# A hybrid decoder step on Trainium2: the opening rearranged, and the dt chain moved between the first blocks of group 0

## The reference

```python
xn = rms_norm(x, norm_mix_w)
u = xn @ w_in                       # 1024 x 10272
glu_v, glu_g, z, xbc, dt_raw, gate_logit = split(u)
a = glu_v * sigmoid(glu_g); a = conv31(a); ...            # convolution branch
xbc = silu(conv4(xbc))                                    # x, B, C of the SSD mixer
dt = softplus(dt_raw + dt_bias)     # 32 heads
A = -exp(a_log)
y, h = ssd(x, dt, A, B, C, h0)      # cumulative sums of dt*A, chunk by chunk (128 tokens)
...
out = (gate0 * y_a + gate1 * y_b) @ w_o
x = x + out; x = x + hier_moe(rms_norm(x))                # 32 experts, top 2
```

## Time and profile before

| | |
|---|---|
| median of 3 runs | 1772.03 us (1767.18 to 1772.23) |
| span of the profiled execution | 1770.0 us |
| TensorE (PE) busy | 1465.9 us, 83% |
| VectorE (DVE) busy | 1348.9 us, 76% |
| ScalarE (ACT) busy | 727.2 us, 41% |
| GpSimd (POOL) busy | 395.0 us, 22% |
| mean granted TensorE clock | 0.903 |

### The profile page before, as it was taken

How to read it: one execution, slowest core, us unless ns; L and a number is a source line. 1 busy time by engine, 2 the same in 40 slices (tenths; PEclk the granted TensorE clock), 3 DMA queues, 4 the chain that set the end, 5 groups by cost and what they waited for, 6 DMA issues and landing times. The chain is left out here.

```text
span 1770.0 us, 27567 instructions
## 1 busy us (share of the span) xinstructions
PE 1465.9 (83%) x8979; PEld 1283.1 (72%) x8979; DVE 1348.9 (76%) x2060; ACT 727.2 (41%) x1012; POOL 395.0 (22%) x467
## 2 busy tenths in 40 slices
PE   3898988989889899898998499998338888888880
PEld 2896887968879688796887389986336777676760
DVE  4169888888888888888888636442738999999984
ACT  3132232322323223232232322332028888888871
POOL 1035243352433424334252000000130000000002
PEclk9599897998989989899799699999669999999995
DMA  4031241411414115141160644320359999999966
GB/s 135 24 96 32 79 107 49 130 44 50 135 47 121 54 45 140 40 128 54 42 179 13 202 143 151 120 78 12 105 210 370 369 372 370 370 371 373 369 241 226
DMA packets 187558, 274.00 MB, mean 155 GB/s; under 512 B 11196, under 2 KB 149670, under 8 KB 172118
## 3 DMA queue, kind: packets, MB, share of 16 engines
q1 hardware_dynamic: 174638, 231.85, 40.0%
q10 hardware_dynamic: 8672, 27.86, 4.0%
q0 software_dynamic: 4208, 13.78, 2.2%
HBM read 224.19 MB, written 50.12 MB: 155 GB/s over the span
## 5 line engine op out<-in xcount | busy, mean ns | idle before, releaser
L731 PE MATMUL pu<-xh,wh 128*128 128x304 f32 (+1 forms) x1280 | 289.2, 309 | 5.8 <-ACT zc L651 4.6
L731 PE MATMUL pu<-xl,wh 128*128 128x304 f32 (+1 forms) x1280 | 279.8, 301 | 0.0
L731 PE MATMUL pu<-xh,wl 128*128 128x304 f32 (+1 forms) x1280 | 278.1, 300 | 0.0
L731 PEld LDWEIGHTS pu<-xh,wh 128*128 128x128 f32 x1280 | 206.9, 199 | 10.2 <-issue 9.9
L731 PEld LDWEIGHTS pu<-xl,wh 128*128 128x128 f32 x1280 | 208.7, 199 | 0.0
L731 PEld LDWEIGHTS pu<-xh,wl 128*128 128x128 f32 x1280 | 206.0, 198 | 0.0
L1965 DVE TENSOR_TENSOR W13l<-W,W13h 128x1024 fp32r<-128x1024 f32 x160 | 185.2, 1221 | 11.3 <-ACT W13h L1913 10.7
L230 POOL TENSOR_TENSOR wl<-ring,wh 128x1024 fp32r<-128x1024 f32 x48 | 118.8, 2475 | 330.2 <-ACT wh L504 330.2
L871 DVE SCALAR_TENSOR_TENSOR cacc<-a_p,gc,cacc 128x528 f32<-128x528 f32 x232 | 187.4, 808 | 0.0
L504 ACT ACTIVATE wh<-ring 128x1024 fp32r<-128x1024 f32 x80 | 84.5, 1057 | 218.4 <-PE pu L731 218.3
L1872 PE MATMUL eh<-W13h,xch 128*128 128x512 f32 x320 | 130.6, 408 | 50.5 <-DVE xcl L1965 46.2
(11 more groups left out here) (381 smaller groups left out, 3195.9 us busy)
## 6 DMA issues: line engine op xcount, KB each, us to landing
W<-in_exp_w SPq DMA_DIRECT2D x120, 1024.0 KB, 8.2
ring<-in_w_in SPq DMA_DIRECT2D x80, 512.0 KB, 3.9
slot_rows<-yo ACTq DMA_DIRECT2D x40, 512.0 KB, 8.6
x<-in_state_ssm SPq DMA_DIRECT2D x16, 512.0 KB, 7.0
out_new_ssm_sample<-x SPq DMA_DIRECT2D x16, 512.0 KB, 5.3
wraw<-in_ssm_out_w SPq DMA_DIRECT2D x8, 1024.0 KB, 8.2
gates<-gbuf ACTq DMA_DIRECT2D x16, 280.0 KB, 2.1
ssd_rows<-yout SPq DMA_DIRECT2D x8, 560.0 KB, 2.9
```

Source lines behind the costliest of these rows:

```text
L731: last = pe.matmul(u_cols(r, a, b), w[:, k % RING, j, :], x[:, j, a:b], start=(j == 0 and n == 0), stop=(j == KD - 1 and n == 2))
```

## The change

- conf_dw_w is loaded by two loads, of 16 and 15 rows (`N_CROW` 19), and the first two weight blocks are issued ahead of dt_bias, a_log and `wdt`. x_prompt comes in four loads, with a semaphore for each tile.
- Square, Sqrt, reciprocal and scaling are done tile by tile; the scaling moves from VectorE to ScalarE. A first Sqrt ahead of the squares loads its table.
- The convolution states are turned into six banks (`state_banks`) of their own, and ScalarE copies them out.
- dt is made with its weights stationary (`dt_rows`): 48 matmuls of 512 or 48 moving columns between blocks 0 and 1 of group 0, with 32 heads on 32 partitions. VectorE copies it to `dtr` after `ssm_conv(0)`, TensorE turns it back in six transposes right behind block 1 (`dt_turned`).
- The rest of the dt chain stands between the steps of group 0: `dt_biased`, `dt_done` and `tails_scaled` behind silu(0), silu(1) and silu(2) on VectorE, `softplus` and `tails` behind silu(0) and silu(1) on ScalarE, `sums_of_a` behind block 3 on TensorE. PoolE's wait for `s_pro` moves behind `split(g, 4)`, with the `ab` copies and `split(g, 5)` behind it.
- Group 0 is written out ahead of the loop on each engine.

```diff
+            for k in range(RING):
+                w_block(0, k)
             sp.dma_start(dtb[:, :], A["dt_bias"][0].partition_broadcast(P)).then_inc(s_dtb, 16)
...
-            pool.wait_ge(s_pro, 1)
...
                 split(g, 4)
+                pool.wait_ge(s_pro, 1)
+                settled(pool)
                 a_over_channels(g, range(3))
...
+            k.link(act.activation(ss[:, 5:6], ss[:, 6:7], ACT.Sqrt))
+            def square(t):
+                S = TILES[t][1]
+                act.wait_ge(s_xt_in[t], 32 if t == 0 else 16)
+                act.activation(ybuf[0:S, :, :].rearrange("p a b -> p (a b)")[:, 0:D], xin[0:S, t, :],
+                               ACT.Square, accum_out=ss[0:S, t:t + 1]).then_inc(s_sq, 1)
+            def root(t):
+                act.wait_ge(s_var, t + 1)
+                act.activation(ss[:, t:t + 1], ss[:, t:t + 1], ACT.Sqrt).then_inc(s_sqrt, 1)
+            def scaled(t):
+                S = TILES[t][1]
+                act.wait_ge(s_inv, t + 1)
+                act.activation(xin[0:S, t, :], xin[0:S, t, :], ACT.Copy, scale=ss[0:S, t:t + 1]).then_inc(s_xs, 1)
...
+            for t in range(len(TILES)):
+                square(t)
+                root(t)
+                scaled(t)
+                if t:
+                    high(2 * t - 2)
+                    high(2 * t - 1)
+                if t == 2:
+                    split(0, 0)
+                if t == 4:
+                    split(0, 1)
+            high(2 * len(TILES) - 2)
+            high(2 * len(TILES) - 1)
...
                 silu(0)
+                if is_first:
+                    softplus()
                 raw(3)
                 silu(1)
+                if is_first:
+                    tails()
                 silu(2)
...
+            def dt_rows():
+                pe.wait_ge(s_wdl, 1)
+                pe.wait_ge(s_sfree, 2)
                 for j in range(KD):
                     for n, (x, w) in enumerate(((xh, wdh), (xl, wdh), (xh, wdl))):
-                        last = pe.matmul(pC[0:S, NH * ci:NH * ci + NH], x[:, j, c:c + S], w[:, j, :],
+                        pe.matmul(pC[0:NH, :], w[:, j, :], x[:, j, 0:512], start=(j == 0 and n == 0), stop=(j == KD - 1 and n == 2))
+                        last = pe.matmul(pY[0:NH, 0:T - 512], w[:, j, :], x[:, j, 512:T],
                                          start=(j == 0 and n == 0), stop=(j == KD - 1 and n == 2))
+                last.then_inc(s_dtm, 1)
+            def dt_turned():
+                pe.wait_ge(s_dtr, 2)
+                for ci, (c, S) in enumerate(CHUNKS):
+                    last = pe.transpose(pC[0:S, NH * ci:NH * ci + NH], dtr[:, c:c + S], ident[0:NH, 0:NH])
+                last.then_inc(s_dtp, 1)
...
+                if is_first:
+                    pe.wait_ge(s_xl, 2 * len(TILES))
                 for k in range(6):
+                    if is_first and k == 1:
+                        dt_rows()
+                        pe.wait_ge(s_sfree, 4)
                     block(k)
+                    if is_first and k == 1:
+                        dt_turned()
+                    if is_first and k == 3:
+                        sums_of_a()
...
+            def dt_copied():
+                dve.wait_ge(s_dtm, 1)
+                dve.tensor_copy(dtr[:, 0:512], pC[0:NH, :]).then_inc(s_dtr, 1)
+                dve.tensor_copy(dtr[:, 512:T], pY[0:NH, 0:T - 512]).then_inc(s_dtr, 1)
...
                 for q in range(4):
                     ssm_conv(q)
+                    if is_first and q == 0:
+                        dt_copied()
                     if q:
                         silu(q - 1)
+                    if is_first and q:
+                        (dt_biased, dt_done, tails_scaled)[q - 1]()
```

More of the change, by code:

```diff
@@ L715, in _, with group @@
+            def group(g, is_first=False):
                 U0 = U_TILES * g
@@ L864, in _ @@
                     last.then_inc(s_u, 1)
+            group(0, is_first=True)
+            with pe.Fori(0, G - 1) as g1:
+                group(g1 + 1)
         @block.vector
@@ L900, in _ @@
             for t, (c, S) in enumerate(TILES):
+                if t + 1 < len(TILES):
+                    variance(t + 1)
                 for h in range(2):
@@ L948, in _, with dt_biased @@
-            dve.wait_ge(s_pro, 1)
-            with dve.Fori(0, G) as g:
-                k.enter(g, DVE_STEPS)
+            dve.wait_ge(s_const, 4)
+            def dt_copied():
+                dve.wait_ge(s_dtm, 1)
+                dve.tensor_copy(dtr[:, 0:512], pC[0:NH, :]).then_inc(s_dtr, 1)
+                dve.tensor_copy(dtr[:, 512:T], pY[0:NH, 0:T - 512]).then_inc(s_dtr, 1)
+            def dt_biased():
+                dve.wait_ge(s_dtb, 32)
+                dve.wait_ge(s_dtp, 1)
+                for ci, (c, S) in enumerate(CHUNKS):
+                    last = dve.tensor_tensor(dtt[0:S, ci, :], pC[0:S, NH * ci:NH * ci + NH], dtb[0:S, :], ALU.add)
+                k.link(last)
+                k.link(dve.tensor_scalar(tmp1[:, :, :], dtt[:, :, :], 0.0, None, ALU.max))
+                stt(tmp2[:, :, :], tmp1[:, :, :], -2.0, dtt[:, :, :]).then_inc(s_dte, 1)
@@ new lines, in dt_done, with tails_scaled @@
+            def dt_done():
+                dve.wait_ge(s_dtl, 1)
+                dve.wait_ge(s_expA, 1)
+                k.link(dve.tensor_tensor(dtt[:, :, :], tmp1[:, :, :], tmp2[:, :, :], ALU.add))
+                stt(aa[:, :, :], dtt[:, :, :], -1.0, expA[:, :].unsqueeze(1).broadcast_to([P, 6, NH]),
+                    ALU.mult, ALU.mult).then_inc(s_a, 1)
+            def tails_scaled():
+                dve.wait_ge(s_aah, 1)
+                k.link(dve.tensor_tensor(aal[:, :, :], aa[:, :, :], aah[:, :, :].bitcast(F32), ALU.subtract))
+                dve.wait_ge(s_te, 7)
+                dve.tensor_tensor(tail[:, :, :], tail[:, :, :], dtt[:, :, :], ALU.mult).then_inc(s_pro, 1)
+                dve.wait_ge(s_pro, 1)
@@ L1107, in _ @@
                 assert next(tap, None) is None
-                k.leave(G)
+            k.enter(0, DVE_STEPS + DT_STEPS)
+            group(0, is_first=True)
+            k.leave(1)
+            with dve.Fori(0, G - 1) as g1:
+                k.enter(g1, DVE_STEPS)
+                group(g1 + 1)
+                k.leave(G - 1)
 OT = [(0, SAMP)] + CHUNKS[2:]
```

193 lines of the change are left out of this document (89 added, 104 removed).

## The result

The changed kernel takes 1757.97 us (median of 4 runs, 1757.03 to 1759.82), beside 1772.13 for the kernel before (4 runs): a ratio of 0.9926, with a 95% interval of 0.9907 to 0.9944, so 14 us faster.

A forecast was written before the change was run, and what follows sets the result against it. The opening was taken as one long chain, with TensorE full through group 0's blocks. Opening -33.4, dt_rows +6.4, behind block 1 +27.0, clock credit 1.5: -1.5 on span 1770.0, 1768.5, so median 1770.5 us; range 1762 to 1779.

The forecast's parts named there:

- the end moves by what the end of block 5 of group 0 moves: Behind block 5 nothing is edited, so the span changes only by the shift of that instant, 0.0 beyond it.
- The clock's credit in the opening: Gapless turnings before block 0 might raise TensorE's clock: state banks up to 1.5, block 0 up to 2.6; 1.5 taken.
- The hold by PoolE: PoolE's subtraction of block 0's low half slows VectorE's tile loop in the opening: 1.2 us added, bounds 0 and 2.4.
- the opening's rest: Opening up to the last x turning: `ds` at 12.4, `cs` ready 18.0, last reciprocal 36.2, last x turning 39.6.
- What comes back behind block 1: Group 0, blocks 1 to 5: TensorE waits at dt_turned and sums_of_a, plus small work, give back 27.0 us.
- Dt_rows: The new dt matmuls between blocks 0 and 1 of group 0 add 6.4 us.
- Block 5 waits for PoolE: Sign in group 0: PoolE's ab copies and split(5) end at E+45.5 (E: block 1's end), about when block 4 ends.
- (a): Rival, chance 0.25: full clock earlier at state banks, block 2 and sums_of_a; -5 to -7.7 us, 1763 to 1765.5.
- (b): Rival, chance 0.12: dt_rows runs at half clock, costing 6.1 there and 2.8 in block 1; 1779.
- (c): Rival, chance 0.06: the edit works as drawn, with no TensorE idle at dt_turned and sums_of_a; 1751.
- (d): Rival, chance 0.05: in the opening `ds` still lands at 18.5 despite the split load; +6, 1776.5.
- The rule that spoke against the change: Skill's rule: a waiting TensorE falls to half clock; without the fall block 2 would be 2.8 shorter, the whole about 1768.

The follow-up runs named there:

- e7: Changed kernel with dt_turned behind block 3, sums_of_a behind block 5 and split(5) ahead of PoolE's wait for s_pro: 1744.88 us, ratio 0.9854.
- e14: Changed kernel with a one-column tanh on ScalarE behind block 0 of groups 1 to 7, asking for an earlier table load: 1763.05 us, ratio 0.9942.
- e15: Kernel before with only ScalarE's group 0 written out ahead of its loop: 1769.11 us, ratio 0.9983.
- e6: Changed kernel with the four large state banks turned ahead of x tiles 3 and 4: 1756.94 us, ratio 0.9904.
- e4: Changed kernel with dt_turned behind block 2 instead of block 1: 1749.86 us, ratio 0.9846.
- e13: Changed kernel run again with no edit, in the last series: 1757.04 us, ratio 0.9914.
- e3: Changed kernel with conf_dw_w in one load of 31 rows again: 1763.06 us, ratio 0.9934.
- e12: Changed kernel with four memsets on VectorE ahead of the first variance, a plain delay: 1766.07 us, ratio 0.9966.
- e8: Changed kernel with normalisation ahead of the constants, four state banks early, dt_turned behind block 3 and sums_of_a behind block 5: 1742.10 us, ratio 0.981.
- e10: Kernel before with only ScalarE's group 0 written out ahead of its loop, on another chip: 1768.18 us, ratio 0.9976.

## Why the prediction was wrong

**Its claim that the end moves by what the end of block 5 of group 0 moves failed.** Block 5 gave 7.9 us in the profiles, the whole 14.7. The forecast assumed that what follows takes as long as before because no line of it is edited. It doesn't: block 5 to root gave 4.9, groups 1 to 7 gave 5.4, and the rest took back 3.5. What follows isn't the same work in the same state. In the kernel before, VectorE is behind when block 5 ends (121.89): only then does it do the last two products of silu, and the first chunk's exp starts on ScalarE at 131.81, 9.9 us behind the end of block 5.

```profile
122.31 1.56 DVE L871 SCALAR_TENSOR_TENSOR cv<-th,cv 128x560 f32<-128x560 f32 x2
...
131.81 0.21 ACT L588 ACTIVATE Lx<-pS 16x64 f32<-16x64 f32 x1 [3.84 <-PE pT L757]
```

In the changed kernel TensorE's two waits let VectorE catch up. It is done with silu at 110.7 and waits 3.82 us, and the first chunk comes 7.3 us behind the end of block 5 (113.98):

```profile
115.70 0.19 DVE L948 SCALAR_TENSOR_TENSOR a_s<-zc 128x32 f32<-128x32 f32 x1 [3.82 <-ACT zc L623]
...
121.28 0.21 ACT L634 ACTIVATE Lx<-pS 16x64 f32<-16x64 f32 x1 [3.19 <-PE pT L817]
```

The sixth chunk's exp starts 43.9 us behind the end of block 5 in all three profiles of the changed kernel, and 47.8, 46.6 and 48.3 us in those of the kernel before: 3.7 of the mean gain of 4.1. In e7, where the waits are gone, it is 47.2 again. So part of what the waits cost ahead of block 5 was work of VectorE that had to be done anyway. The rest goes with the clock: behind block 5 the granted clock is 0.94 instead of 0.87. In groups 1 to 7 a short group has about 14 us at the 1.2 GHz level and a long one about 20; what sets how many groups are short isn't shown. The table load's place is a candidate that the runs don't confirm: the edit in e14 cost 6 us in the changed kernel, the one in e15 gained nothing in the kernel before. The prediction never looked at table loads behind the opening, and the edit that moved them, writing group 0 out, was counted at nothing without a word.

Of the 13.2 us by which the span was forecast too long (-1.5 against -14.7), this step has 6.8; the other 6.4 lie ahead of the end of block 5, in the next two points. Either part alone would have left the time inside the range.

**The clock's credit in the opening was mis-sized.** It was 1.5 of at most 4.1. The state banks, with TensorE turning without a pause from 36.8 on, took the times of the full level (1.18 for sixteen of 24 columns, where 1.87 is that of the half) and ended at 44.2 instead of 47.5: 5.1 us for all six instead of 7.9. Even the bound of 1.5 on the banks was too low by the prediction's own row, in which turnings of 1.09 take 0.63: on 7.9 us that is 3.3. The durations decide here, since the view shows a granted clock of 1.00 for 31.0 to 38.9 as well, where turnings of 128 columns still take 1.11; the trace's first record of the clock is at 41.7. Block 0 took 7.8 instead of 8.9. So the clock gave 3.9 where 1.5 was credited. The hold by PoolE, charged at 1.2, came (1.82 instead of 0.69), but beside the banks, where it costs nothing, and the banks began 0.5 earlier. Together block 0 ended 5.8 us before the forecast's time without credit, 4.3 more than was credited. e6 shows what the other price was: with a pause in front, the same small turnings take 1.87. Of the opening's rest, the terms stood: the copy of `ds` starts at 13.5 (forecast 12.4), `cs` is scaled by 19.0 (18.0), the last reciprocal 35.4 (36.2), the last x turning ends at 39.1 (39.6).

**What comes back behind block 1 had the right mechanism.** From the end of block 1: ssm_conv(0) starts at 4.1 (forecast 4.2), `dtr` is done at 8.5 (8.9), block 2 ends at 18.1 (18.9), sums_of_a starts at 30.7 (31.9), PoolE's `ab` copies start at 38.5 (39.7) and take 2.10 (3.34), block 5 ends at 49.4 (51.6), the remaining 2.2 us. Dt_rows took 6.4, as taken. e4 shows that taking the first wait away brings 6.5 us in time, and e7 that taking away both brings 12.2 (against e13, on the same chip), at the price of new waits of 2.3 and 5.9. "Block 5 waits for PoolE" didn't come: PoolE was done at 107.5, just when block 4 ended at 107.75.

**The rivals.** (a), the kinder clock, is nearest: it named the banks, block 2 and the sums. The banks came, and part of block 0; block 2 and the sums didn't (granted clock 0.68 in block 2 with the turnings, the sums 2.13 us behind a wait and 1.23 without one). It would have ended at 1763 at best, because it too stopped at block 5. (b) is wrong: the granted clock was 1.00 in dt_rows. (c) was no rival of this order, but is what e7 makes of it: 1744.9. (d) is wrong, and e3 shows that it would have cost 6.7.

**The rule that spoke against the change**, that a TensorE that is kept waiting starts its next tile cold, held: block 2 took 8.8 us behind a wait of 8.63 (9.5 with the turnings) and 6.2 behind none (e4). It was rightly in the sum; what was missed is that the opening, too, had lost such a pause.

**What stays open.** Why a group becomes long or short; whether the table load's place matters to it, since in the kernel before it didn't change the time; and why e12's median moved by more than its delay. The 3 us that come back behind the last root are open too, but they aren't chance: this stretch takes 793.0 to 793.9 us in all five profiles of the kernel before with and without ScalarE's group 0 written out, and 796.1 to 797.3 in twelve of the thirteen of the changed kernel and its variants (803.4 in e8), wherever the table load stands. In the first two profiles they are in the experts (425.1 and 428.4 us from their first weights to their last tanh).

## What to carry to other kernels

When an edit moves the start of a long loop or writes out its first pass, don't take the rest of the loop as fixed: ask which engine is behind at the point where the forecast stops, since a wait ahead of it gives that engine time to catch up; compare several passes by their length and granted clock, and look where the instructions stand that the compiler puts in, such as table loads. A chain over several engines that is threaded between blocks costs TensorE nothing only if each of its steps stands as many blocks late as the chain ahead of it needs; count that from the end of the block that frees the weight slot, and place the step behind the first block that ends later. Before small work is moved into an earlier pause, ask whether it closes a pause where it stands: in e6 the move gained nothing.

## What the runs showed of the hardware

- In one execution, passes of one loop with the same instructions take 109.7 or 112.4 us, at granted clocks of 0.94 and 0.91 and with TensorE busy 98.9 and 101.5 us.
- With group 0 of ScalarE's loop written out, the compiler put the table load of 1.28 us ahead of the first tanh of each group instead of its head (e10, e15). A tanh that draws the load into ScalarE's idle time came with 6 us more in the changed kernel (e14); the cause isn't shown.
- One load of 31 rows, in place of 16 and 15, delayed the load of `ds` behind it by 4.9 us (e3).
- A GpSimd subtraction of 2.9 us on 1024 columns held a VectorE subtraction of 512 columns for 1.82 us instead of 0.69.
- Sixteen turnings of 24 columns take 1.18 us behind a run of large turnings and 1.87 behind a pause of 2.26 us.
